# Hybrid decoder layer on one core: the first expert's loads and item table issued at other places, and the second tile of x loaded ahead of the latents' weights

## What is computed

```
h     = RMSNorm(x);  proj = h @ W_in    # latents (416 columns), pool channels (512), gates (2 x 1024)
x     = x + (sigmoid(g_a) * attention + sigmoid(g_p) * pooling) @ W_o
x     = x + MoE(RMSNorm(x))             # 32 experts, 4 for each token
x     = x + sigmoid(RMSNorm(x) @ W_gate) * (p @ W_ple)

MoE: logits -> top 4 -> softmax gates; for each expert, on its tokens:
     gu = xb @ w_gate_up[e] + b;  act = (up + 1) * gate * sigmoid(1.702 * gate)   # both clamped at 7
     y  = act @ w_down[e] + b
```

## Time and profile before

| | us |
|---|---|
| median of 3 runs (2413.55 to 2413.87) | 2413.63 |
| the profiled execution | 2407.64 |
| its span, first to last instruction | 2406.0 |
| PE busy in the span | 2365.7 (98%) |
| DVE, ACT, POOL busy | 1333.8, 459.0, 422.2 |
| mean granted TensorE clock | 0.997 of full |

### The profile page before, as it was taken

The page is one execution under the profiler, slowest core; times in us unless marked ns, Lnnn a source line. Parts: engine busy times, 40 slices in busy tenths (PEclk is TensorE's granted clock), DMA queues, the critical chain, the costliest instruction groups (busy, mean ns, idle before and its releaser), DMA issues. The chain is left out here.

```text
span 2406.0 us, 45416 instructions
## 1 busy us (share of the span) xinstructions
PE 2365.7 (98%) x15707; PEld 1612.7 (67%) x15707; DVE 1333.8 (55%) x2479; ACT 459.0 (19%) x1148; POOL 422.2 (18%) x589
## 2 busy tenths in 40 slices
PE   8999999999998999999999999999999999999999
PEld 6765664444444888888888888888656565655544
DVE  4665674111356554455445554556767676776565
ACT  3434552000022100000000000100212222121332
POOL 2451102121243310001100111110110101011230
PEclk9999999999999999999999999999999999999999
DMA  5000002312052898888888888888999899999462
GB/s 151 27 18 10 1 0 53 122 26 52 27 178 88 271 378 319 284 293 293 288 301 307 286 300 314 302 305 324 329 337 356 325 359 339 343 346 338 160 201 88
DMA packets 255034, 531.84 MB, mean 221 GB/s; under 512 B 17846, under 2 KB 67910, under 8 KB 254951
## 3 DMA queue, kind: packets, MB, share of 16 engines
q1 hardware_dynamic: 222302, 472.57, 55.4%
q0 software_dynamic: 17440, 38.97, 5.2%
q10 hardware_dynamic: 15208, 19.14, 2.2%
HBM read 498.76 MB, written 31.87 MB: 221 GB/s over the span
## 5 line engine op out<-in xcount | busy, mean ns | idle before, releaser
L1937 PE MATMUL banks<-arena_a,arena_w 128*128 128x144 f32 (+7 forms) x4608 | 568.4, 286 | 2.2 <-ACT arena_a L2109 2.2
L1937 PEld LDWEIGHTS banks<-arena_a,arena_w 128*128 128x128 f32 x4608 | 564.6, 190 | 9.0 <-issue 6.5
L1990 PE MATMUL banks<-arena_w,arena_a 128*64 128x256 f32 x2688 | 298.6, 380 | 3.0 <-DVE arena_a L2268 1.7
L1990 PEld LDWEIGHTS banks<-arena_w,arena_a 128*64 128x64 f32 x2688 | 193.3, 137 | 107.2 <-issue 14.1
L2363 DVE TENSOR_SCALAR arena_m<-banks,arena_m 128x160 f32<-128x160 f32 x144 | 55.3, 384 | 302.8 <-PE banks L1937 302.3
L2164 ACT ACTIVATE arena_m<-arena_m 128x160 f32<-128x160 f32 x144 | 48.5, 337 | 789.0 <-DVE arena_m L2363 474.3
L1305 POOL DMA_DIRECT2D arena_m<-slot_tokens x32 | 18.7, 585 | 1026.6 <-issue 1026.6
L1945 PE MATMUL banks<-arena_w,arena_a 128*64 128x256 f32 x1728 | 197.5, 381 | 0.0
L2046 PE MATMUL banks<-arena_w,arena_a 128*128 128x512 f32 x448 | 194.6, 592 | 0.0
L1945 PEld LDWEIGHTS banks<-arena_w,arena_a 128*64 128x64 f32 x1728 | 120.9, 137 | 67.6 <-issue 10.4
L2046 PEld LDWEIGHTS banks<-arena_w,arena_a 128*128 128x128 f32 x448 | 84.0, 190 | 100.4 <-issue 100.4
(11 more groups left out here) (411 smaller groups left out, 3440.9 us busy)
## 6 DMA issues: line engine op xcount, KB each, us to landing
arena_w<-in_w_gate_up_dram SPq DMA_DIRECT2D x128, 2048.0 KB, 12.7
arena_w<-in_w_down_dram SPq DMA_DIRECT2D x32, 4096.0 KB
expert_rows<-arena_a ACTq DMA_DIRECT2D x104, 128.0 KB, 9.3
arena_a<-in_x_dram SPq DMA_DIRECT2D x16, 512.0 KB, 4.9
arena_w<-in_w_in_dram SPq DMA_DIRECT2D x16, 512.0 KB, 5.4
arena_a<-in_b_down_dram SPq DMA_DIRECT2D x14, 512.0 KB, 15.3
expert_rows<-arena_a ACTq DMA_DIRECT2D x28, 192.0 KB
arena_a<-in_b_down_dram SPq DMA_DIRECT2D x72, 64.0 KB
```

Of the source, the lines that this page charges most:

```text
L1937: m = pe.matmul(GU[f % 3][:, to:to + width], w[c][:, k, at:at + P], xT[:, k, 0:width], start=(k == 0), stop=(k == K - 1), skip_group_check ...
L1990: m = pe.matmul(at[h * TH:(h + 1) * TH, :], x[:, k, :], w[:, k, h * QB:(h + 1) * QB], start=(start and k == 0), stop=(stop and k == KH - 1 ...
```

## The change

Five edits go together. (1) At the program's start x of tile 1 is issued ahead of both halves of `w_lat`. (2) Of half c = 1 of expert 0's gate and up weights, three quarters (all of `wg[1]`, and the lower half of `wu[1]`) are issued within `route`'s loop on SP, ahead of the stores of tile T - 2, behind a wait for product 5 of the last pair; the last quarter (1 MB) stays where the whole was. Since that half now counts 48 on its semaphore, the waits for c = 1 are 16 higher. (3) The item table is written and read back by ACT's queue, between the copies of item 0's rows and its sigmoids; SP goes straight on to the down weights. (4) 30 transposes instead of 10 stand ahead of the last tile's ranks on PE. (5) 10 more stand behind them.

```diff
@@ front, SP
                         sp.dma_start(gain_row[:, :], g_mix[0].partition_broadcast(P)).then_inc(sem("gain"), 16)
+                        sp.dma_start(xt[1], x2d[P:2 * P, :]).then_inc(sem("x1"), 16)
                         for h in (0, 1):
                             rows = slice(h * D // 2, (h + 1) * D // 2)
                             sp.dma_start(w_lat[:, 4 * h:4 * h + 4, :], w_in[rows, 0:LAT].rearrange("(k p) n -> p k n", p=P)).then_inc(sem(f"w_lat{h}"), 16)
-                            if h == 0:
-                                sp.dma_start(xt[1], x2d[P:2 * P, :]).then_inc(sem("x1"), 16)
@@ route, SP
+        gate_second, up_second = (w_gate_up[0][:, at:at + CW].rearrange("(k p) n -> p k n", p=P) for at in (CW, FF + CW))
...
+                    if n == T - 2:
+                        sp.wait_ge(out_done, made(PAIRS - 1, 5))
+                        sp.dma_start(wg[1], gate_second).then_inc(w_gu_here[1], 16)
+                        sp.dma_start(wu[1][:, 0:KH, :], up_second[:, 0:KH, :]).then_inc(w_gu_here[1], 16)
...
                 sp.wait_ge(out_done, 7 * PAIRS)
                 sp.wait_ge(rows_here, 32)
-                load_gate_up(sp, 0, 1)
+                sp.dma_start(wu[1][:, KH:K, :], up_second[:, KH:K, :]).then_inc(w_gu_here[1], 16)
@@ route, PE
                 logits(T - 1)
+                stay_warm(WARM * 3 // 4)
+                ranks(T - 1)
                 stay_warm(WARM // 4)
-                ranks(T - 1)
@@ experts, SP
-                sp.wait_ge(sem("fields"), 1)
-                sp.dma_start(item_dram, fields_i[0:ITEM_ROWS, :]).then_inc(sem("table"), 16)
-                sp.wait_ge(sem("table"), 16)
-                sp.dma_start(items[:, :], item_dram.rearrange("(o i) f -> o (i f)", o=1)).then_inc(sem("table"), 16)
                 load_down(sp, 0)
@@ experts, PE and DVE, three places
-                            wait_value(pe, w_gu_here[c], 32 * i + 32)
+                            wait_value(pe, w_gu_here[c], 32 * i + (32 + 16 * c))
@@ experts, ACT
                 keep_x(0)
+                act.wait_ge(sem("fields"), 1)
+                act.dma_start(item_dram, fields_i[0:ITEM_ROWS, :]).then_inc(sem("table"), 16)
+                act.wait_ge(sem("table"), 16)
+                act.dma_start(items[:, :], item_dram.rearrange("(o i) f -> o (i f)", o=1)).then_inc(sem("table"), 16)
                 expert_item(0)
```

More of the change, by code:

```diff
@@ L2271, in sum_w1 @@
                     b11, b12, b21, b22 = quarters(c)
-                    wait_value(dve, w_gu_here[c], 32 * i + 32)
+                    wait_value(dve, w_gu_here[c], 32 * i + (32 + 16 * c))
                     if c:
```

## The result

| | before | changed |
|---|---|---|
| median of 20 runs each, side by side | 2412.59 us (2408.32 to 2414.77) | 2416.88 us (2411.59 to 2423.24) |
| ratio, 95% interval | 1 | 1.0019 [1.0013, 1.0025] |
| profiled execution | 2407.64 us, span 2406.0, clock 0.997 | 2421.46 us, span 2419.9, clock 0.993 |

The kernel became slower by 0.19%, where 2409.3 us (4.35 us faster) was forecast, with a range up to 2412.3. In both traces what follows the start of item 1's gate and up takes the same time: to the end of the span it is 2406.0 - 848.17 = 1557.8 us before and 2419.9 - 862.24 = 1557.7 after. So everything happened ahead of that mark, and it can be counted.

A forecast was written before the change was run, and what follows sets the result against it. PE's stream was taken as the bound, so only single waits or slow stretches could go. Start -0.8, transposes with early load -0.6, table -2.95, gate and up 0: -4.35 us from 2413.63 to 2409.3, range 2407.2 to 2412.3.

The forecast's parts named there:

- Part 1: Program start: x of tile 1 ahead of the latents' weights gains 0.8 us, from 1.5 gain to 0.1 loss.
- By then the same bytes have passed: Program start: the worst landing of `w_lat`'s first half is 13.1, when x landed before; 11.3 at best.
- it carries through the front, as PE is its bound: Front: the 0.8 us gained at the start was to last through the front.
- Part 2: Last ranks: added transposes fill idle time and hold the clock, 44 taking 5 to 5.7 us; -0.6 together with early load.
- the rival: Around the last ranks: the added transposes don't hold the clock, the 0.6 is lost, 2409.9 us; chance 0.07.
- Part 3: Last pair: 3 MB loaded early in 8.5 us beside POOL's scatters; -0.6 together with the transposes, ends -1.2 and +0.2.
- the next groups move by up to 3.6 us: POOL's scatters beside the early load: a group lands within 8.3 us instead of 4.70.
- Gate and up: Item 0's gate and up: the slow stretch that cost 1.7 us stays, so 0, ends -1.7 and +1.7.
- Part 4: Item table on ACT: first transfer takes 6 us, so item 1's wait goes in full, -2.95 us.
- the slow rival: Table starves on ACT beside SP's loads, PE stalls at block 5; with 20 and 5 us, 2421.7 us; chance 0.05.
- its 18.2 us from POOL's list to item 1's turn: Time from POOL's release to PE's turn of item 1's rows, used to place those rows.
- a rival with 0.12: Item table no sooner: first transfer takes 11.7 us on ACT too, the 2.95 us wait stays, 2412.2 us; chance 0.12.

The follow-up runs named there:

- the second profile: The changed kernel with all five edits, run and profiled once more, against the kernel before: 2411.88 us, ratio 1.0015.
- the second run of the early load: Edit 2 alone against the kernel before, run again on another chip: 2401.70 us, ratio 0.9974.
- with the down weights held: Edits 2 to 5, with SP issuing expert 0's down weights only once the item table is back, against the kernel before: 2406.54 us, ratio 0.9989.
- the third group: Runs on one chip, kernel before at 2407.91 us: edit 2 again 2401.70, edits 2, 4, 5 2402.27, these with 24 start transposes 2401.55, edit 1 with 26 transposes 2409.45.
- the first group: Runs on another chip, kernel before at 2408.15 us: edit 1 alone 2411.35, edits 2 to 5 2410.38, edit 2 alone 2405.73, edit 3 alone 2414.20.
- with the scatters held: Edits 2 to 5, with POOL's last 8 scatters held until the item table is back, executed once: 2425.52 us, item 1's list late by design.

## Why the prediction was wrong

**What bounds.** Right: the change could only move single waits and slow stretches, and that is all that moved.

**Part 1 (forecast -0.8, ends -1.5 and +0.1).** No gain in any run, and a loss in the changed kernel. x of tile 1 was no longer waited for, as said. The step that failed is the landing of `w_lat`'s first half: I had 11.3 at best and 13.1 at worst and took the middle; PE could start on it at 13.4, with the edit alone at 13.1, in the second profile at 13.3. "By then the same bytes have passed" was the true account, and the slow clock behind the wait then costs the first half 1.7 to 2.9 us. Its pool channels began at 21.3 to 22.9 against my 20.1 to 21.7. The best end was wrong as well: "it carries through the front, as PE is its bound" is false, since the next wait, the heads' for DVE, takes back what an earlier start gives. In six of the ten traces with before's order of loads the pool channels began at 19.7 to 20.2, and the front's mix was no earlier for it (53.6 to 54.6, against 53.6 to 54.1 in the four with a start at 21.1 to 21.6). Measured cost of the edit: 1.1 and 1.3 us at the front's mix in the two profiles of the change, 0.2 in that of the edit alone, which is within the spread of before's order.

**Part 2 (transposes).** The mechanism came as forecast in seven of the eight traces with these edits, and against the rival: clock 1.00 from 775 to 785 and 44 transposes in 5.00 us; in the profile of the change the last ranks stand straight behind the choice (a wait of 0.24). In the second profile of the change it failed: 7.95 us. By the Trainium skill, TensorE: Matmul & The Clock Gate, PE-mode transpose, they should have had no effect; the runs disagree with it: in the profile of the change PE did little but transposes from 775 to 785, and the clock stood at 1.00. What was mis-sized is the gain: the turn waits for its rows and item 1's turn for the table, so by themselves they gave 0 (ratio 1.0002).

**Part 3 (early load, forecast -0.6 with part 2, ends -1.2 and +0.2).** The failed step is "the next groups move by up to 3.6 us": I costed one group of scatters. POOL's wait for the group beside the load was 5.7 to 10.5 us in the nine traces that have it and 4.7 to 7.3 in the five that don't, and the wait for the next group 5.5 to 8.6 against 4.7 to 5.7. In the profile of the change they were 10.54 and 7.62 us. POOL's slack ahead of the gather was about 3 us, and the gather fell 10.6 us behind, of which 2.7 stood ahead of this place already (1.1 from the front, 1.6 from the clock at 200). Not all of the rest, 7.9 us, belongs to the load: POOL was 2.0 us late, beyond the 2.7, before the load was issued at 753.04. Reckoned in the same way the eight other traces with the early load show -0.6 to 2.2, and in six of them DVE released the gather and no scatter. So the price was up to 2.2 us in eight traces, though not shown to be the scatters' each time, and 7.9 in one. The load itself also did not take 8.5 us at 369 GB/s: in the second run of the early load its first 2 MB landed after 13.0 us, and beside the scatters of 762 to 766 DMA moved 133 GB/s at a share of 0.91 in the profile of the change.

**Gate and up (forecast 0, ends -1.7 and +1.7).** Right by its bounds where the records have no break: 36.72 in the run of the transposes alone and 36.62 with the early load besides, 38.08 with the down weights held, and 35.04, without a slow stretch, in the second run of the early load alone. In the changed kernel's first profile the two parts take 23.41 + 15.90 = 39.3 us without the break, 2.6 over before's 36.72 and past the upper end, because the clock fell behind the break too; in the second 22.00 + 14.98 = 37.0.

**Part 4 (forecast -2.95).** The step that failed most: "I take 6, nearer to the first, because the long one stood behind megabytes of its own queue." An empty queue of its own did not help. The transfer needs 4.2 to 6.3 us on SP and 6.5 on ACT when no bulk load is beside it, 7.9 on ACT beside the down weights alone, and 16.0 to 19.5 on ACT when the down weights and the last tiles' scatters both are. (Before, with bulk load and scatters too, it took 11.2 to 11.9 on SP in four traces; how much of that was the queue no run separates.) The change itself put the down weights there, by letting SP go on without the table. The other false step stands next to it: "1 MB, 4 MB and the bias take some 15 us, to 803", the argument against the slow rival. The 4 MB alone landed 27.4 us after their issue in the profile of the change. And `fields`, which the prediction had at 797.0, was ready at 806.6 there and at 801.0 in the second profile. Most of that rival was worked out right: ACT's sigmoids are queued behind the wait, PE stalls at block 5 with landings of 16.0 us and more and does not with 7.9, and the break is after 160 records in every such trace, 2.35 to 4.89 us long. Wrong was its 18.2 us from POOL's list to item 1's turn: with the down weights past by then it was 15.0 to 15.9 in the changed kernel's second profile and the runs of edits 2 to 5 and of the table alone, so item 1's rows cost 0 to 1.2 us and not 9.5. I gave it 0.05; it was the case that came, milder than with my 20 and 5 us.

That a sooner table takes away the wait is right: with the early load alone item 1's wait of 2.95 fell to 0 and 0.80. But edit 2 does that without edit 3, since it takes three of the four megabytes out of the way of SP's queue. The Trainium skill, DMA: Bandwidth & Descriptors, Rules for kernel authors, says that spreading transfers over queues saves issue time only, as the DMA engines behind them are the same. The traces agree: 6.3 us on SP, 6.5 on ACT in like surroundings. I had named it as a rival with 0.12 and without the second half, that the new place's wait stops an engine with work queued.

**The sum.** By single edits: start +0.12%, table +0.25%, transposes 0, early load -0.08 and -0.26%; the whole +0.19 and +0.15%. Each of these has an interval of about 0.1% to either side. The version to keep is the early load with table and start as they were: three kernels with it, with or without the transposes, lie at 2401.6 to 2402.3 us against 2407.9 in the third group; in the first group its gain of 2.4 us is at the edge of noise.

**What stays open.** Why the clock falls at 200 us in some executions; why the start alone lost 3 us in the median while its one profile lost 0.2; and why the early load gained 2.4 us in one group and 6.2 in another (chip, scatters or clock). Why scatters and bulk load slow each other no run shows. Whether the last scatters could be moved out of the way of the down weights without delaying item 1's list was not tried.

## What to carry to other kernels

Before a small transfer that others wait for is moved to another queue, ask what will be in flight beside it, and above all what the move itself lets loose: here the wait that was taken from SP had been holding 4 MB back. A wait for a transfer belongs on an engine that has nothing queued behind it. And carry a gain at the start through to the next wait behind it, before it goes into a sum.

## What the runs showed of the hardware

Indirect scatters of 4-byte elements and a bulk load hinder each other far beyond their bytes. In the changed kernel, with both in flight, the DMA engines stayed at a share of 0.94 to 1.06 and moved 107 and 151 GB/s, against 395 to 415 GB/s for the same load with the scatters held; 4096-byte packets took up to 2.33 us in the mean of two microseconds instead of 0.16; and a table of 3 KB took 16.0 to 19.5 us instead of 7.9 beside the load alone and 4.2 to 6.5 without it.

The granted clock may fall or not behind the same wait of PE: after 1.04 us at about 200 us it stayed at 1.00 in eight traces and fell in six, for 1.5 us of time. And a stretch of unused transposes ran at 1.00 in seven traces (44 in 5.00 us) and met a fall to 0.50 in one (7.95 us).
